# Gate marks two expert units sooner, and the dot products of one token group spread anew, in a mixed-attention and expert-layer kernel

## The chip, the cores and the metric

The kernel runs on one core of one Trainium2 chip. The metric is the device time of one launch in microseconds. Besides the timed runs there is one profiled execution, whose rows are quoted below: PE is the matmul engine (PEld its weight loads), DVE the vector engine, ACT the scalar engine, POOL the GpSimd engine, SP the engine that only issues transfers.

## The reference

One layer: four attention branches over 512 tokens, a merge, a layer norm, and then the expert layer (PEER) that this change is about. Cut to that:

```python
q = (xt @ wq).reshape(t_len, 8, 2, 64)
sub = einsum('thpd,hpkd->thpk', q, subkeys)        # 128 keys per half
s_top, i_top = top_k(sub, 16)
cand = s_top[:, :, 0, :, None] + s_top[:, :, 1, None, :]
sc, ci = top_k(cand.reshape(t_len, 8, 256), 16)
eid = (i1 * 128 + i2)                               # 8 heads x 16 = 128 experts a token
gate = softmax(sc, axis=-1)
h = gelu(einsum('cd,ced->ce', xc, u[eid]))          # u: 16384 x 1024
out = einsum('ce,ced->cd', gate * h, v[eid])
```

Everything is float32; the kernel splits each float32 operand into a high and a low part and adds three products.

## The kernel before

**Two ways through the expert layer.** Tokens 128 to 511 (three groups of 128) are computed densely: 128 "expert units" multiply all 16384 rows of `u` with the 384 tokens, 24 matmuls a unit (three per 128 columns, lines 1444 to 1446). After each unit ACT applies gelu (`gelu_of`, L776) and stores 192 KB of it to memory (`gelu_d`, L788); the store of unit j has to land before the gelu of unit j + 2 may write the same buffer (L785). The last eight units, 120 to 127, keep their gelu on the chip and store nothing. Then 128 "value units" multiply gate times gelu with `v`. Tokens 0 to 127 go another way: for each of their 128 picks one row of `u` per token is gathered by POOL (`get_u`, L535, an indirect transfer of 512 KB) and DVE takes a dot product with it (`dot`, L1168). The dot products have no dependence on the matmuls of the units, and are spread over the units as filler for DVE.

**Routing and marks.** DVE finds the picks of each token group (`route(b)`), b = 0 first and then 1, 2, 3. `route` calls `between` after each of its steps, 21 times in all, and there the dot products and marks of the previous stretch are slipped in (`next_units`, L1400). When route(b) is done, PE turns the picks round (three transposes, `turn_picks`, L1800) behind the unit before `MARK_AT[b]`, DVE copies them (`spread_picks`, L1290), and then a gate table for the 384 tokens is built eight tokens at a time: DVE makes a one-hot pair `hits` and `right` (`mark`, L1303), and PE multiplies them (`gates_of`, L1806, 16 matmuls a group, between two units). There are 48 such groups, 16 for each b. ACT copies the result to `stage` and, when four groups are full, stores four pieces of 512 KB to `gate_d` (`store_gates`), one piece a unit. For the last four groups it stores all four pieces at once, behind unit `TAIL`.

**What sets the order.** `MARK_AT` holds the unit at which each stretch of marks starts, and (entry 4, `TAIL`) the one after its end: `groups_in(j)` says which groups belong to unit j. `DOT_PACE` holds how many dot products are done by which unit; `dots_by(j)` (L84) interpolates between its points. PE, DVE, ACT and POOL all unroll their order from these tables:

- DVE does route(1) in the units 16 to `MARK_AT[1]` - 1, route(2) in the first stretch of marks, route(3) in the second.
- POOL makes the low part of each unit's weights (`expert_lo(k)`, L528, for unit k + 2) and between two of them issues gathers. The first 15 rows use three buffers, one row a unit; from `MARK_AT[1]` on it issues up to `dots_by(k - 1) + 5` rows before `expert_lo(k)`, in five buffers. Each gather waits until the dot product that last used its buffer is done (L535 and following), and row 15 also for the end of route(1). In a unit with a group, POOL waits in addition for that group's `right` (L570).
- ACT runs the exponent of each group's gates at a fixed unit, with a table load ahead of it and one behind it (`gate_exp`, L821, called at L838).
- SP loads the weights of the units one after the other, and after that of unit 125 the first part of the gate table.

```python
for k in range(FIRST_UNITS, MARK_AT[1]):
    expert_lo(k)
    rows_to(min(EARLY, k - FIRST_UNITS + 1))
for k in range(MARK_AT[1], P):
    rows_to(dots_by(k - 1) + U_SLOTS)
    if groups_in(k):
        pool.wait_ge(right_set, groups_in(k).stop)
    expert_lo(k)
```

Of the kernel before, what the change touches and what calls it, by code (L numbers as in the profile page):

```python
# [25 lines left out]
P = 128  # L26
# [43 lines left out]
GATE_SCALE = 2.0 ** 15  # L70
FIRST_UNITS = 16
STEPS = 22
MARK_AT = {1: 31, 2: 62, 3: 93, 4: 115}
TAIL = MARK_AT[4]
DOT_PACE = ((FIRST_UNITS + 5, 0), (MARK_AT[1], 14), (MARK_AT[2], 49), (MARK_AT[3], 84), (TAIL, 114), (P - 3, P))
EARLY, EARLY_SLOTS = 15, 3
U_SLOTS, V_SLOTS = 5, 6
FMA_START, FMA_END = 2, P - 12
# [5 lines left out]
def dots_by(k):  # L84

    for (k0, n0), (k1, n1) in zip(DOT_PACE, DOT_PACE[1:]):
        if k < k1:
# [4 lines left out]
def groups_by(b, k):  # L92

    return P // MARKED * (b - 1) + P // MARKED * k // (MARK_AT[b + 1] - MARK_AT[b])


def groups_in(j):

    b = marking_at(j)
    return range(groups_by(b, j - MARK_AT[b]), groups_by(b, j - MARK_AT[b] + 1)) if b else range(0)  # L100

# [7 lines left out]
def marking_at(j):  # L109

    return sum(j >= MARK_AT[b] for b in range(1, NT)) if j < TAIL else 0

# [87 lines left out]
def peer_block(nc, xT, x_rows, w_units, u_units, v_rows, u_rows, sinks, ln1_g, ln1_b, subk, ln2_g, ln2_b,  # L200
# [182 lines left out]
    with nc.Block() as block:  # L383
# [90 lines left out]
        def _(pool):  # L474
# [53 lines left out]
            def expert_lo(k):  # L528

                n = U_EXP + k + LO_AHEAD  # L530
                pool.wait_ge(hi_done, n + 1)
                pool.tensor_tensor(w_lo[:, n % RAW, :], raw[:, n % RAW, :], w_hi[:, n % RAW, :].bitcast(F32),  # L532
                                   ALU.subtract).then_inc(lo_pool, 1)
# [21 lines left out]
            def rows_to(n):  # L555
                while got[0] < min(n, P):
                    get_u(got[0])
                    got[0] += 1
# [4 lines left out]
            rows_to(EARLY_SLOTS)  # L563
            for k in range(FIRST_UNITS, MARK_AT[1]):
                expert_lo(k)
# [1347 lines left out]
```

## Time and profile before

| what | value |
|---|---|
| median of 3 runs | 1657.44 us (1654.45 to 1659.41) |
| the profiled execution's own time | 1661.09 us |
| its span | 1659.4 us |
| PE busy | 1636.9 us, 99% of the span |
| DVE / ACT / POOL busy | 74% / 42% / 51% |
| mean granted PE clock | 0.997 |
| chain that ended last | PE 86%, DVE 8%, DMA 2% |

PE is busy for nearly the whole span, so what a change is worth is read from the few gaps between its matmuls and from the stretches in which its clock is not full. All times below are in us from the start of the span. The expert units run from about 544 to 1128.

### The profile page before, as it was taken

The page shows a single profiled execution, that of the slowest core. Times are in us where ns is not written, and L with a number is a line of the kernel's source. Part 1 is how long each engine was busy: PE and PEld are TensorE (multiplying, and loading weights), DVE is VectorE, ACT ScalarE, POOL GpSimd, SP SyncE. Part 2 cuts the span into 40 slices and gives each one's busy share as a digit, 9 for nine tenths or more (in the row PEclk, how much of TensorE's full clock was granted, in tenths as well). Part 3 has the DMA queues.
Part 4 walks back from the last instruction along what each step waited for, and adds up shares of the span by engine and source line. Part 5 has one row for each costly group of instructions (what it writes and reads, how often), then busy time and mean ns, then how long its engine had stood idle before and what let it go on. Part 6 is the DMA issues. An engine that isn't in the chain of part 4 may idle for free.

```text
span 1659.4 us, 24178 instructions
## 1 busy us (share of the span) xinstructions
PE 1636.9 (99%) x9013; PEld 1436.7 (87%) x9013; DVE 1230.8 (74%) x2375; ACT 692.4 (42%) x1030; POOL 840.6 (51%) x492
## 2 busy tenths in 40 slices
PE   9999999999999999999999999999999999999997
PEld 7778777788889999999999999998888888888886
DVE  3586895512162988999899978736988888888886
ACT  4556545523233444444444544433333333333342
POOL 6232232444461568787887899873532233223212
PEclk9999999999999999999999999999999999999999
DMA  5121122233331568998999999999999999999952
GB/s 209 64 77 52 53 86 66 89 127 115 117 114 62 155 213 293 311 341 322 356 354 334 334 344 400 356 349 357 399 394 356 361 386 357 370 386 346 387 186 89
DMA packets 131684, 417.62 MB, mean 252 GB/s; under 512 B 13552, under 2 KB 33008, under 8 KB 131568
## 3 DMA queue, kind: packets, MB, share of 16 engines
q1 hardware_dynamic: 70320, 232.81, 40.0%
q0 software_dynamic: 36864, 134.23, 21.8%
q10 hardware_dynamic: 24384, 49.03, 7.7%
q8 instruction: 72, 1.18, 0.3%
q14 instruction: 44, 0.36, 0.1%
HBM read 364.91 MB, written 50.86 MB: 251 GB/s over the span
## 4 chain that ended last, share of the span: by engine, by line
PE 86%; DVE 8%; DMA 2%; ACT 1%; POOL 1%; issue 1%; ACTq 0%; SPq 0%; DVEq 0%
PE ps L1444 16%; PE ps L1445 16%; PE ps L1446 16%; PE ps L1706 10%; PE ps L1703 10%; PE ps L1704 10%; PE ps L1815 2%; DVE u_got L1168 1%; DVE hits L1311 1%; PE ps L1556 1%; PE ps L1508 1%; DMA gelu_d<-gelu_t 1%; POOL w_lo L488 1%; PE ps L1539 1%; DVE right L1318 1%
## 5 line engine op out<-in xcount | busy, mean ns | idle before, releaser
L1444 PE MATMUL ps<-tok_hi,w_hi 128*128 128x384 f32 (+1 forms) x1472 | 526.3, 358 | 4.0 <-ACT gelu_t L786 3.7
L1446 PE MATMUL ps<-tok_hi,w_lo 128*128 128x384 f32 (+1 forms) x1472 | 517.7, 352 | 0.0
L1445 PE MATMUL ps<-tok_lo,w_hi 128*128 128x384 f32 (+1 forms) x1472 | 517.6, 352 | 0.0
L595 ACT ACTIVATE w_hi<-raw 128x1024 fp32r<-128x1024 f32 x330 | 349.2, 1059 | 396.8 <-PE ps L1706 293.0
L532 POOL TENSOR_TENSOR w_lo<-raw,w_hi 128x1024 fp32r<-128x1024 f32 x128 | 312.8, 2444 | 109.1 <-ACT w_hi L595 66.6
L488 POOL TENSOR_TENSOR w_lo<-raw,w_hi 128x1024 fp32r<-128x1024 f32 x76 | 182.0, 2399 | 314.7 <-ACT w_hi L595 314.5
L1444 PEld LDWEIGHTS ps<-tok_hi,w_hi 128*128 128x128 f32 x1472 | 276.7, 188 | 34.1 <-issue 10.3
L549 POOL DMA_INDIRECT v_got<-v_rows,eid x128 | 153.1, 1196 | 300.9 <-DVE own L1180 283.7
L1703 PE MATMUL ps<-w_hi,gh_hi 128*128 128x512 f32 x760 | 295.7, 389 | 0.0
L1704 PE MATMUL ps<-w_lo,gh_hi 128*128 128x512 f32 x760 | 295.7, 389 | 0.0
L1446 PEld LDWEIGHTS ps<-tok_hi,w_lo 128*128 128x128 f32 x1472 | 276.9, 188 | 18.1
L1445 PEld LDWEIGHTS ps<-tok_lo,w_hi 128*128 128x128 f32 x1472 | 277.1, 188 | 16.0
L1706 PE MATMUL ps<-w_hi,gh_lo 128*128 128x512 f32 x760 | 234.0, 389 | 0.0
L1162 DVE TENSOR_TENSOR w_lo<-raw,w_hi 128x1024 fp32r<-128x1024 f32 x126 | 156.4, 1241 | 74.3 <-ACT w_hi L595 74.2
L1168 DVE CUSTOM_DVE_ANT_0 u_got<-u_got,ps 128x1024 f32<-128x1024 f32 x128 | 153.0, 1216 | 50.0 <-DMA u_got<-u_rows,eid 47.3
L1706 PEld LDWEIGHTS ps<-w_hi,gh_lo 128*128 128x128 f32 x760 | 142.6, 188 | 29.7
L1703 PEld LDWEIGHTS ps<-w_hi,gh_hi 128*128 128x128 f32 x760 | 142.7, 188 | 29.6
L1704 PEld LDWEIGHTS ps<-w_lo,gh_hi 128*128 128x128 f32 x760 | 142.6, 188 | 29.6
L541 POOL DMA_INDIRECT u_got<-u_rows,eid x128 | 155.5, 1215 | 25.0 <-issue 15.8
L1180 DVE SCALAR_TENSOR_TENSOR own<-v_got,w_own,own 128x1024 f32<-128x1024 f32 x126 | 160.0, 1279 | 0.0
L786 ACT ACTIVATE gelu_t<-ps 128x384 f32<-128x384 f32 x120 | 59.1, 492 | 228.6 <-PE ps L1446 211.8
L1311 DVE TENSOR_TENSOR hits<-numbers,mark_keys 128x2048 f16<-128x2048 f16 x48 | 94.8, 1974 | 0.8
(248 smaller groups left out, 1782.2 us busy)
## 6 DMA issues: line engine op xcount, KB each, us to landing
raw<-u_units SPq DMA_DIRECT2D x128, 512.0 KB
raw<-v_rows SPq DMA_DIRECT2D x128, 512.0 KB
raw<-w_units SPq DMA_DIRECT2D x78, 512.0 KB
gate_d<-stage ACTq DMA_DIRECT2D x48, 512.0 KB
gelu_d<-gelu_t ACTq DMA_DIRECT2D x120, 192.0 KB
gelu_in<-gelu_d SPq DMA_DIRECT2D x30, 768.0 KB, 8.1
gate_in<-gate_d SPq DMA_DIRECT2D x28, 768.0 KB, 12.3
gate_in<-gate_d SPq DMA_DIRECT2D x2, 1536.0 KB, 12.3
```

Source lines behind the costliest of these rows:

```text
L488: pool.tensor_tensor(lo_of(n), raw[:, n % RAW, :], hi_of(n).bitcast(F32), ALU.subtract).then_inc(lo_done, 1)
L532: pool.tensor_tensor(w_lo[:, n % RAW, :], raw[:, n % RAW, :], w_hi[:, n % RAW, :].bitcast(F32), ALU.subtract).then_inc(lo_pool, 1)
L595: act.activation(hi_of(n), raw[:, n % RAW, :], ACT.Copy).then_inc(hi_done, 1)
L1162: dve.tensor_tensor(w_lo[:, n % RAW, :], raw[:, n % RAW, :], w_hi[:, n % RAW, :].bitcast(F32), ALU.subtract).then_inc(lo_dve, 1)
L1168: dve.tensor_tensor_reduce(out=u_got[row_slot(e)][:], in0=u_got[row_slot(e)][:], in1=ps[:, 6:8, :].rearrange("p a n -> p (a n)"), scale=1. ...
L1180: dve.scalar_tensor_tensor(own[e % 2][:], v_got[e % V_SLOTS][:], w_own[:, e:e + 1], own[e % 2][:], ALU.mult, ALU.add).then_inc(fma_done, 1)
L1444: pe.matmul(out_, l_hi, r_hi, start=start, stop=False)
L1445: pe.matmul(out_, l_hi, r_lo, start=False, stop=False)
L1446: return pe.matmul(out_, l_lo, r_hi, start=False, stop=stop)
L1703: pe.matmul(o, l_hi[:, tile_], wh, start=start, stop=False)
L1704: pe.matmul(o, l_hi[:, tile_], wl, start=False, stop=False)
L1706: last = pe.matmul(o, l_lo[:, tile_], wh, start=False, stop=stop)
```

## The change

Each stretch of marks starts two units sooner (29, 60, 91 in place of 31, 62, 93) and the last one ends two units sooner (its last group at unit 112 in place of 114). The points of `DOT_PACE` hang on `MARK_AT`, so they move with it, and each count is 3 lower: 11 dot products by unit 29 (14 by 31 before), then 35, 35 and 30 in the stretches (as before), and 17 in the last 15 units (14 in the last 13 before). `EARLY`, the number of buffers, and every instruction are as they were; only the order changes. The names used elsewhere are unchanged.

```diff
-MARK_AT = {1: 31, 2: 62, 3: 93, 4: 115}
+MARK_AT = {1: 29, 2: 60, 3: 91, 4: 113}
 TAIL = MARK_AT[4]
-DOT_PACE = ((FIRST_UNITS + 5, 0), (MARK_AT[1], 14), (MARK_AT[2], 49), (MARK_AT[3], 84), (TAIL, 114), (P - 3, P))
+DOT_PACE = ((FIRST_UNITS + 5, 0), (MARK_AT[1], 11), (MARK_AT[2], 46), (MARK_AT[3], 81), (TAIL, 111), (P - 3, P))
```

POOL around the start of the marks, before. The rows begin with the low part of unit 30's weights (`expert_lo(28)`); u_got_143 to u_got_145 are the three buffers of the first rows, with 146 and 147 the five of the later ones.

```order
L532 TENSOR_TENSOR w_lo<-raw,w_hi 128x1024
L541 DMA u_got_143<-u_rows,eid 128x1024
L532 TENSOR_TENSOR w_lo<-raw,w_hi 128x1024
L541 DMA u_got_144<-u_rows,eid 128x1024
L532 TENSOR_TENSOR w_lo<-raw,w_hi 128x1024
L541 DMA u_got_145<-u_rows,eid 128x1024
L541 DMA u_got_146<-u_rows,eid 128x1024
L541 DMA u_got_147<-u_rows,eid 128x1024
L541 DMA u_got_143<-u_rows,eid 128x1024
L541 DMA u_got_144<-u_rows,eid 128x1024
L532 TENSOR_TENSOR w_lo<-raw,w_hi 128x1024
```

POOL at the same place, of the change; the first row is again the low part of unit 30.

```order
L532 TENSOR_TENSOR w_lo<-raw,w_hi 128x1024
L541 DMA u_got_143<-u_rows,eid 128x1024
L541 DMA u_got_144<-u_rows,eid 128x1024
L541 DMA u_got_145<-u_rows,eid 128x1024
L541 DMA u_got_146<-u_rows,eid 128x1024
L532 TENSOR_TENSOR w_lo<-raw,w_hi 128x1024
L541 DMA u_got_147<-u_rows,eid 128x1024
L532 TENSOR_TENSOR w_lo<-raw,w_hi 128x1024
```

Behind the low part of unit 30, rows 12 to 15 (buffers 143 to 146) now stand together ahead of the low part of unit 31. Before, row 12 and row 13 each stood before one low part, and rows 14 to 18 together ahead of that of unit 33.

DVE at the end of route(1), before: from the last step of the routing (L1286 sets the picks) to the first group of marks (L1311, L1318). Each L1168 pair is one dot product.

```order
L1286 TENSOR_TENSOR pick<-pick,g_sum 128x128
L1168 ISA u_got_145,h_own<-u_got_145,ps 128x1024
L1168 ISA h_own 128x1
L1168 ISA u_got_143,h_own<-u_got_143,ps 128x1024
L1168 ISA h_own 128x1
L1168 ISA u_got_144,h_own<-u_got_144,ps 128x1024
L1168 ISA h_own 128x1
L1296 CAST mark_keys<-ps 128x256
L1297 TENSOR_SCALAR mark_gates<-ps 128x64x2
L1299 SCALAR_TENSOR_TENSOR mark_gates<-ps,mark_gates 128x64x2
L1192 MAX s_top<-sub 128x8 x8
L1168 ISA u_got_145,h_own<-u_got_145,ps 128x1024
```

This piece is word for word the same in the change; its dot products are those of rows 8, 9, 10 and, behind the copy of the picks, 11, where before they are 11, 12, 13 and 14. Route(1) itself holds 8 dot products in the change and 11 before, since three of them drop out of its steps: here is one place of the difference.

```order
 L1268 TENSOR_TENSOR sub<-c_row,ps 128x2048
-L1168 ISA u_got_145,h_own<-u_got_145,ps 128x1024
-L1168 ISA h_own 128x1
-L1168 ISA u_got_143,h_own<-u_got_143,ps 128x1024
-L1168 ISA h_own 128x1
 L1272 TENSOR_TENSOR sub<-sub,ps 128x2048
+L1168 ISA u_got_144,h_own<-u_got_144,ps 128x1024
+L1168 ISA h_own 128x1
 L1275 TENSOR_REDUCE pick<-sub 128x128
```

ACT behind the last group of marks (`stage` is the copy of the gates, `gate_d` the four pieces stored at once): the difference.

```order
 L801 ACTIVATE stage_138<-ps 128x128x4 x2
 L809 DMA gate_d<-stage_138 128x1024 x4
+L595 ACTIVATE w_hi<-raw 128x1024
+L786 ACTIVATE gelu_t<-ps 128x384
+L788 DMA gelu_d<-gelu_t 128x384
+L595 ACTIVATE w_hi<-raw 128x1024
+L786 ACTIVATE gelu_t<-ps 128x384
+L788 DMA gelu_d<-gelu_t 128x384
 L595 ACTIVATE w_hi<-raw 128x1024
 L786 ACTIVATE gelu_t<-ps 128x384
```

Two more gelus, each with a store, follow the four pieces: six (units 114 to 119) in place of four (116 to 119) before the units that store nothing.

## Rows read from the trace of the kernel before

**Rows 1.** The page's first part: busy time and share of each engine.

```profile
PE 1636.9 (99%) x9013; PEld 1436.7 (87%) x9013; DVE 1230.8 (74%) x2375; ACT 692.4 (42%) x1030; POOL 840.6 (51%) x492
```

**Rows 2.** PE's waits by releaser, the longest: us in total, times, longest.

```profile
PE ps L1444 <- ACT gelu_t L786: 3.7, 1, 3.7
```

**Rows 3.** Stretches: busy us (instructions) of each engine, clock, DMA share, GB/s.

```profile
588.00:661.50 73.50, 73.50 (x426) 73.50 (x426) 63.35 (x239) 29.94 (x40) 55.74 (x31) 1.00 0.81 263
...
677.00:762.00 85.00, 84.42 (x580) 82.59 (x579) 83.61 (x251) 37.58 (x55) 68.06 (x39) 1.00 0.93 331
```

**Rows 4.** Timeline of PE: start, us, operation [idle before <- releaser].

```profile
668.42 0.49 PE L1803 MATMUL ps<-ident,pick 128*128 128x128 f32 x3
...
676.92 0.34 PE L1446 MATMUL ps<-tok_hi,w_lo 128*128 128x384 f32 x1
677.31 1.09 PE L1815 MATMUL ps<-right,hits 128*128 128x128 f16 x16
...
761.02 0.34 PE L1446 MATMUL ps<-tok_hi,w_lo 128*128 128x384 f32 x1
761.88 1.10 PE L1815 MATMUL ps<-right,hits 128*128 128x128 f16 x16 [0.53 <-DVE right L1318]
```

**Rows 5.** Timeline of DVE, end of route(1) and first marks.

```profile
625.23 1.22 DVE L1168 CUSTOM_DVE_ANT_0 u_got<-u_got,ps 128x1024 f32<-128x1024 f32 x1 [7.93 <-DMA u_got<-u_rows,eid]
...
659.23 2.34 DVE L1286 TENSOR_TENSOR pick<-pick,g_sum 128x128 f32<-128x128 f32 x1
...
668.27 1.22 DVE L1168 CUSTOM_DVE_ANT_0 u_got<-u_got,ps 128x1024 f32<-128x1024 f32 x1 [3.14 <-DMA u_got<-u_rows,eid]
...
669.42 0.42 DVE L1296 CAST mark_keys<-ps 128x256 f16<-128x256 f32 x1
...
671.96 1.21 DVE L1168 CUSTOM_DVE_ANT_0 u_got<-u_got,ps 128x1024 f32<-128x1024 f32 x1
...
676.03 1.22 DVE L1318 TENSOR_TENSOR right<-hits,mark_gates 128x2048 f16<-128x2048 f16 x1
```

**Rows 6.** Timeline at the start of the third stretch, PE and then DVE.

```profile
958.90 0.49 PE L1803 MATMUL ps<-ident,pick 128*128 128x128 f32 x3
...
959.43 0.42 DVE L1296 CAST mark_keys<-ps 128x256 f16<-128x256 f32 x1 [4.74 <-issue]
```

**Rows 7.** Timeline of POOL around the start of the marks.

```profile
659.01 2.40 POOL L532 TENSOR_TENSOR w_lo<-raw,w_hi 128x1024 fp32r<-128x1024 f32 x1
661.57 0.95 POOL L541 DMA_INDIRECT u_got<-u_rows,eid  x1 [0.16 <-issue]
...
667.59 0.94 POOL L541 DMA_INDIRECT u_got<-u_rows,eid  x1 [0.30 <-issue]
668.84 0.93 POOL L541 DMA_INDIRECT u_got<-u_rows,eid  x1 [0.31 <-issue]
```

**Rows 8.** Timeline of ACT and its queue behind unit 115.

```profile
1072.09 0.49 ACT L786 ACTIVATE gelu_t<-ps 128x384 f32<-128x384 f32 x1 [3.14 <-PE ps L1446]
...
1074.10 3.10 ACTq L809 DMA_DIRECT2D gate_d<-stage  x4
...
1078.77 0.33 ACTq L788 DMA_DIRECT2D gelu_d<-gelu_t  x1
...
1081.15 0.49 ACT L786 ACTIVATE gelu_t<-ps 128x384 f32<-128x384 f32 x1 [0.89 <-DMA gelu_d<-gelu_t]
...
1091.84 0.49 ACT L786 ACTIVATE gelu_t<-ps 128x384 f32<-128x384 f32 x1 [8.68 <-DMA gelu_d<-gelu_t]
```

**Rows 9.** Timeline of PE at the end of unit 119.

```profile
1088.36 0.34 PE L1446 MATMUL ps<-tok_hi,w_lo 128*128 128x384 f32 x1
1092.39 0.45 PE L1444 MATMUL ps<-tok_hi,w_hi 128*128 128x384 f32 x1 [3.69 <-ACT gelu_t L786]
```

**Rows 10.** The stretch behind that gap, columns as in rows 3.

```profile
1093.60:1097.00 3.40, 3.40 (x12) 3.40 (x11) 1.23 (x2) 1.80 (x3) 2.92 (x2) 0.50 1.00 330
```

**Rows 11.** Timeline of DVE ahead of the value units.

```profile
1120.19 0.56 DVE L1344 TENSOR_TENSOR gh_lo<-gh,gh_hi 128x384 fp32r<-128x384 f32 x1 [8.63 <-ACT gh_hi L851]
```

## The prediction

> **What bounds the kernel now.** I read the page's busy times first: PE is busy for 99% of the span [rows 1], so only three things can move the time: a gap between matmuls, a stretch at the lower clock, or a different number of matmuls. The change has the same instructions, so the third is out. The list of PE's waits comes next: the longest of all is one wait of 3.7 us for a gelu [rows 2]. Then the timeline of PE, for the place and size of each gap in the expert units [rows 4, 9]. A unit is 24 matmuls and takes (1088.70 - 1072.05) / 4 = 4.16 us, from the end of unit 115 (ACT's gelu behind it starts at 1072.09 [rows 8]) to that of unit 119 (1088.36 + 0.34 [rows 9]): one matmul starts 0.17 us behind the other. What is beyond that is lost:
>
> - At unit 32, with the first group of marks: 676.92 to 677.31, less 0.17: 0.22 us.
> - At unit 50: 761.02 to 761.88, less 0.17: 0.69 us, waiting for `right`.
> - Ahead of unit 120: 1088.36 to 1092.39, less 0.17: 3.86 us, waiting for ACT's gelu of unit 118. Behind it, from 1093.6, stand 3.40 us at a granted clock of 0.50, which is 1.2 GHz of the 2.4 [rows 10]; they hold half the work, so they cost 1.70 us. Together 5.56 us.
>
> So there is 0.91 us at the start of the marks and 5.56 us in the tail to win, and whatever is delayed by more than its slack to lose. From 677 to 762 DVE is busy for 83.61 of 85 us [rows 3]: in the first stretch it has no room, and its work there starts with the copy of the picks.
>
> **The front: picks and marks two units sooner.** PE asks for the picks of group 1 not at 668.42 [rows 4] but at 668.42 - 8.32 = 660.1. DVE had them at 659.23 + 2.34 = 661.6 [rows 5]. With nothing else changed, PE would wait 1.5 us. But route(1) now holds 8 dot products and not 11, each 1.15 us to the next instruction (668.27 to 669.42 [rows 5]): 3.45 us less, and the picks are there at 658.1, 2 us ahead. Besides, DVE idled for 73.5 - 63.35 = 10.2 us of that stretch [rows 3], 7.93 of it for row 3 [rows 5]. POOL issues these rows at the same units as before and the dot products stand later in the routing, so DVE is there later and waits less; of the 10.2 us I take 6 to 7 away: picks at about 652. The dot products of rows 8, 9 and 10 follow. Row 13 was issued at 661.57 [rows 7] and used at 668.27, 6.7 us later; row 10 goes out three units sooner, at some 649 to 651, and is there by 657.5. So DVE is free before 659 and waits for the transposes. At the third stretch, where it waited too, the copy starts 959.43 - 958.90 = 0.53 us behind the first transpose [rows 6]; at the first stretch it was 669.42 - 668.42 = 1.00, because the dot product at 668.27 was late by 3.14 us [rows 5]. In the change the copy then starts at 660.1 + 0.53 = 660.6, 0.47 us sooner against PE. From the copy to the end of the first `right` are 676.03 + 1.22 - 669.42 = 7.83 us: 668.5. PE comes to that group 676.92 + 0.17 - 668.42 = 8.67 us behind its transposes, at 668.8: no wait. Up to unit 50 DVE has the same instructions from the copy on, so the 0.91 us that PE lost shrinks by 0.47 to about 0.44. **Gain 0.47 us.** Bounds: 0.91 if both gaps go; a loss of 0.4 if DVE's waits don't shrink, since the three dot products then end at 658.1 + 3.45 = 661.5, 0.9 behind 660.6.
>
> **POOL at the same place.** This is a wait that the change adds. Ahead of the low part of unit 31 now stand rows 13, 14 and 15, and row 14 goes into the buffer of row 11, whose dot product stands behind the copy of the picks. It ends 671.96 + 1.15 - 669.42 = 3.69 us behind the start of the copy [rows 5]: 664.3. Until then POOL stands still, and the low part of unit 31, SP's load into the buffer that it frees, and all later gathers queue behind it. Then come rows 14 and 15 at 1.25 us each (667.59 to 668.84) and the low part of 2.40 us [rows 7]: 664.5 + 2.5 + 2.4 = 669.4. Unit 31 starts when unit 30 and the first group (1.09 us busy [rows 4], some 0.9 to 1.0 until the next unit's matmul) are done: 668.8 + 0.95 = 669.7. It fits by 0.3 us, where before this low part was ready at 659.01 + 2.40 = 661.4 [rows 7], over 7 us ahead. I take 0, the row nearest to it being on time; bounds 0 and 1 us. Unit 32 needs one row and one low part more: 669.4 + 3.65 = 673.1 against 669.7 + 4.16 = 673.9, and then the slack grows, since 3.65 us a unit is less than 4.16.
>
> **Exponent, middle.** ACT's exponent with its table loads moves with the marks to unit 24, which ends at 660.1 - 4 x 4.16 = 643.5; it has until DVE is within some 3 us of the picks (649), and it is three short instructions. From the second stretch on groups and dot products lie as before, two units sooner, and DVE has room there (4.74 us of idle at the third copy [rows 6]). 0 us for both; if that cover were gone, each us would be one on PE.
>
> **The tail.** Where the 3.86 us come from [rows 8]: behind unit 115 ACT issues the four pieces of 512 KB in one go (1074.10, 3.10 us), then the gelu store of unit 116 (1078.77). That lies behind 2 MB in the same queue and is landed at 1091.8, 13.0 us later; gelu 118 waits 8.68 us for it, and PE with it. In the change the pieces go out behind unit 113, and the store of unit 114 lies behind them. Dot products in the units that follow have the same sequence (1, 1, 2, 1, 2, 1, 1, 2, 1, 2), so the gathers on the DMA are the same too. With t for the end of the unit with the four pieces (1072.05), the store is issued at t + 6.7 and lands at t + 19.8, and PE wants the bank at t + 16.6: the same wait, ahead of unit 118. **Change 0 us**; bounds -5.56 (it lands 4 us sooner) and +5.2 (a rival below). The three dot products that came in end with unit 124 as before, and DVE idles 8.63 us ahead of the value units [rows 11], which hides them (3.45 us).
>
> One rule of the Trainium skill bears on the 1.70 us. The rows: behind 3.86 us of idle the clock fell to 1.2 GHz [rows 9, 10]. The page "TensorE: Matmul & The Clock Gate" (Part 1: The HAM clock gate) says that the activity window is free-running, so the same kernel shows different numbers of slow matmuls from run to run. By the row the moved gap costs the 1.70 again; by the rule it may cost none of it, and the sum would be 1655.3 in place of 1657.0. No run here shows which.
>
> **Sum.** The profiled execution took 1661.09 us (span 1659.4 and 1.7 around it): -0.47 at the marks, 0 elsewhere: 1660.6. It is 3.65 us over the median of the runs shown, which may be a part of the tail's 5.56. On the median: 1657.44 - 0.47 = **1657.0 us**.
>
> **Rivals.**
>
> *The tail wait goes.* For: the store before it landed 8.5 us after its issue (1072.6 to 1081.1 [rows 8]), and 13.0 need to fall by only 3.9. Against: the same 2 MB in the same queue. 1657.44 - 5.56 - 0.47 = 1651.4.
>
> *A second wait in the tail*, the one that ends slower. Before, the units behind the waiting gelu 118 are 119, behind which PE shows no gap, and 120, which stores nothing. In the change gelu 118 must wait for the store of unit 116, issued behind the first wait at t + 20.3. PE comes to unit 120 at t + 20.3 + 4.16 + 1.7 + 4.16 = t + 30.3. If the store takes 8.5 us, gelu 118 is done at t + 29.3, in time by 1 us; from 9.5 us on it is late, and at 13.0 it costs 3.5 us and 1.7 of slow clock: +5.2, less 0.47: 1662.2. For: the DMA's share there is 1.00 [rows 10]. Against: the 2 MB are gone by then.
>
> *POOL stands still too long on dot product 11.* It decides from 0.3 us on, and each us is one on PE at unit 31: with 1.5 us 1658.5.
>
> *The picks are late.* PE waits at unit 28, the 1.5 us worked out above: 1658.9. Against: the three dot products fewer.
>
> **How the numbers follow.** The forecast 0.62, the tail wait gone 0.15, the second wait 0.11, the two small delays 0.12 together. About 0.3% (5 us) is what a measurement of this kernel can tell from no change; the runs of before spread over as much. Below it lies only the first rival, with a little for parts unseen: faster 0.17. Above it only the second: slower 0.15. Same 0.68. Range 1652 to 1662: the forecast with the spread of the runs, the small delays, and part of each large case.
>
> **What would show it.** In the changed profile: the copy of the picks at about 660.6 with over 1 us of idle ahead of it; the first group, at unit 30, with no gap; the gap at unit 48 under 0.5 us; POOL's standstill on a dot product ahead of row 14, and unit 31 without a gap; ACT's wait for `gelu_d` of 5 us or more at gelu 116 and PE's gap of 3 to 4 us ahead of unit 118, with a stretch at 0.5 clock behind it. The prediction is wrong if PE has no gap over 2 us in the tail, or two, or if one over 1 us stands between units 28 and 33.

## The result and the profile after

| | median, us | lowest to highest | runs |
|---|---|---|---|
| before | 1655.56 | 1654.45 to 1659.41 | 22 |
| after | 1658.39 | 1656.63 to 1664.60 | 22 |

The ratio after to before is 1.0022, with a 95% interval of 1.0016 to 1.0028. By the medians the change is slower by 2.83 us (1.0017), by the means by 3.40 us, since six runs of after and none of before lie above 1660; the account below is of the medians. The loss lies inside the 0.3% that I had called no difference, but with this many runs it is clearly told from none, and it goes the other way than the 0.47 us that I forecast. One run of e8 and one of e15, below, took 4207 us in a slow state, and they stand outside the ratios and move those medians by some 0.02 us.

The number I started from was off as well. The median of the three runs shown was 1657.44; over 22 runs it is 1655.56. The profiled execution of before (1661.09) is 5.53 us above that: just the 5.56 us of [rows 8 to 10]. So the tail wait in the profile seems to belong to single runs and not to the typical one; e15 below bears that out (0.62 us of it in the median). The profiled execution of after (1658.28) is near its median.

The page's busy times and the list of PE's waits, after (answers to [rows 1, 2]; us in total, times, longest):

```profile
PE 1635.9 (99%) x9013; PEld 1436.4 (87%) x9013; DVE 1232.7 (74%) x2375; ACT 691.4 (42%) x1030; POOL 840.7 (51%) x492
...
PE ps L1815 <- DVE right L1318: 2.8, 2, 1.6
PE ps L1630 <- POOL ident L483: 1.6, 1, 1.6
PE ps L1444 <- DVE m_lo L1055: 1.4, 1, 1.4
PE ps L1444 <- ACT gelu_t L786: 1.2, 1, 1.2
```

The instructions are the same in number. Two waits on `right` have come, 2.8 us in all where there was one of 0.5, and the wait for a gelu is down from 3.7 to 1.2. PE's timeline, after (start, us, operation [idle before <- releaser]; answers to [rows 4, 9]):

```profile
659.18 0.49 PE L1803 MATMUL ps<-ident,pick 128*128 128x128 f32 x3
...
669.66 1.03 PE L1815 MATMUL ps<-right,hits 128*128 128x128 f16 x15 [1.65 <-DVE right L1318]
...
754.83 1.09 PE L1815 MATMUL ps<-right,hits 128*128 128x128 f16 x16 [1.12 <-DVE right L1318]
...
1082.84 0.44 PE L1444 MATMUL ps<-tok_hi,w_hi 128*128 128x384 f32 x1 [1.19 <-ACT gelu_t L786]
```

From start to start, less the 0.17 us of one matmul, the gaps are 1.81 us at the first group (0.22 before), 1.29 us at the tenth (0.69 before) and 1.36 us in the tail (3.86 before, with 1.70 of half clock). The two at the front make 3.10 us in place of 0.91: **+2.19 us**. Why the first `right` is late stands in the timelines of DVE and POOL, after (answers to [rows 5, 7]):

```profile
655.85 1.22 DVE L1168 CUSTOM_DVE_ANT_0 u_got<-u_got,ps 128x1024 f32<-128x1024 f32 x1 [3.67 <-DMA u_got<-u_rows,eid]
...
659.71 0.42 DVE L1296 CAST mark_keys<-ps 128x256 f16<-128x256 f32 x1 [2.62 <-PE ps L1803]
...
662.25 1.20 DVE L1168 CUSTOM_DVE_ANT_0 u_got<-u_got,ps 128x1024 f32<-128x1024 f32 x1
...
665.05 1.23 DVE L1311 TENSOR_TENSOR hits<-numbers,mark_keys 128x2048 f16<-128x2048 f16 x1
666.31 3.29 DVE L1318 TENSOR_TENSOR right<-hits,mark_gates 128x2048 f16<-128x2048 f16 x1
```

```profile
654.41 2.40 POOL L532 TENSOR_TENSOR w_lo<-raw,w_hi 128x1024 fp32r<-128x1024 f32 x1
...
658.22 0.94 POOL L541 DMA_INDIRECT u_got<-u_rows,eid  x1 [0.31 <-issue]
663.73 0.93 POOL L541 DMA_INDIRECT u_got<-u_rows,eid  x1 [4.57 <-DVE h_own L1168]
664.97 0.94 POOL L541 DMA_INDIRECT u_got<-u_rows,eid  x1 [0.30 <-issue]
665.93 2.58 POOL L532 TENSOR_TENSOR w_lo<-raw,w_hi 128x1024 fp32r<-128x1024 f32 x1
```

Row 14 waits 4.57 us for dot product 11. So the low part of unit 31 starts at 665.93, just ahead of `right` at 666.31, and `right` takes 3.29 us where it took 1.22 [rows 5]. It ends at 669.60, 1.09 us behind the end of POOL's instruction (668.51). Before, that low part ran from 659.01 [rows 7], and no POOL arithmetic lay beside the first `right` (676.03 to 677.25). POOL's low parts around it, before:

```profile
671.03 2.41 POOL L532 TENSOR_TENSOR w_lo<-raw,w_hi 128x1024 fp32r<-128x1024 f32 x1
...
677.33 2.40 POOL L532 TENSOR_TENSOR w_lo<-raw,w_hi 128x1024 fp32r<-128x1024 f32 x1 [2.78 <-DVE right L1318]
```

The tail, ACT and its queue, after (answers to [rows 8]):

```profile
1065.04 0.49 ACT L786 ACTIVATE gelu_t<-ps 128x384 f32<-128x384 f32 x1 [3.15 <-PE ps L1446]
...
1067.05 3.05 ACTq L809 DMA_DIRECT2D gate_d<-stage  x4
...
1071.67 0.33 ACTq L788 DMA_DIRECT2D gelu_d<-gelu_t  x1
...
1082.30 0.49 ACT L786 ACTIVATE gelu_t<-ps 128x384 f32<-128x384 f32 x1 [6.92 <-DMA gelu_d<-gelu_t]
```

The store behind the four pieces lands 10.6 us after its issue (1071.67 to 1082.3), where before's took 13.0. The wait is where I put it, and smaller.

### The profile page after: what moved, and what is told of

It reads as the page before. It is cut to its first block, busy times and chain, and to the rows that moved or that the text cites. A ratio compares the mean times of both kernels' runs of the same rounds, so it can differ in the third digit from the quotient of the medians.

```text
span 1656.5 us, 24176 instructions
## 1 busy us (share of the span) xinstructions
PE 1635.9 (99%) x9013; PEld 1436.4 (87%) x9013; DVE 1232.7 (74%) x2375; ACT 691.4 (42%) x1030; POOL 840.7 (51%) x492
## 4 chain that ended last, share of the span: by engine, by line
PE 91%; DVE 4%; DMA 2%; ACT 1%; POOL 1%; issue 0%; ACTq 0%; SPq 0%; DVEq 0%
PE ps L1444 18%; PE ps L1446 17%; PE ps L1445 17%; PE ps L1704 10%; PE ps L1706 10%; PE ps L1703 10%; PE ps L1815 3%; PE ps L1556 1%; PE ps L1508 1%; POOL w_lo L488 1%; PE ps L1539 1%; DMA gelu_d<-gelu_t 1%; DMA raw<-w_units 1%; DMA x_raw<-xT 0%; DVE right L1318 0%
## 5 line engine op out<-in xcount | busy, mean ns | idle before, releaser
L1168 DVE CUSTOM_DVE_ANT_0 u_got<-u_got,ps 128x1024 f32<-128x1024 f32 x128 | 153.1, 1216 | 44.9 <-DMA u_got<-u_rows,eid 44.3
L1311 DVE TENSOR_TENSOR hits<-numbers,mark_keys 128x2048 f16<-128x2048 f16 x48 | 95.1, 1982 | 0.8
```

## The experiments

Each was timed in five rounds beside the kernel before, on the same chip; the changed kernel was not timed in these rounds, so it is set beside them by its own +2.83 us over before. The intervals are about 1.5 us wide to either side, so a difference of medians below that is a hint, and the readings rest on the traces. The gaps are those of the one profiled run, whose time stands behind the median (from start to start, less 0.17 us): those of e3, e6 and e9 are 1.3, 2.7 and 3.4 us above their medians.

| run | marks; dots | median; profiled run | before there | ratio, 95% interval | gaps of PE: first group, tenth, tail |
|---|---|---|---|---|---|
| e1_front | 29, 60, 91, 115; 11, 46, 81, 114 | 1656.91; 1656.91 | 1655.34 | 1.0008, 0.9999 to 1.0017 | 1.81, 1.25, none |
| e2_tail | 31, 62, 93, 113; 14, 49, 84, 111 | 1655.01; 1656.48 | 1655.34 | 0.9997, 0.9988 to 1.0006 | 0.51, 0.72, 1.08 |
| e3_dots | 31, 62, 93, 115; 11, 46, 81, 111 | 1660.19; 1661.44 | 1655.34 | 1.0030, 1.0021 to 1.0039 | 1.82, 0.95, 2.50 and slow clock |
| e4_lofirst | as after | 1656.09; 1655.95 | 1655.34 | 1.0007, 0.9998 to 1.0016 | none, 0.81, 0.98 |
| e5_early14 | as after | 1657.64; 1657.15 | 1655.37 | 1.0013, 1.0004 to 1.0022 | none (1.11 at the second group), 1.45, 0.73 |
| e10_taildots | as before, 111 by the last | 1656.61; 1656.61 | 1655.66 | 1.0003, 0.9994 to 1.0012 | 0.59, 0.71, 0.59 |
| e6_spaced | as after | 1657.65; 1660.36 | 1655.66 | 1.0010, 1.0001 to 1.0018 | 1.81, 1.31, 1.30 and 1.19 |
| e8_best | as after | 1655.45; 1654.76 | 1655.66 | 1.0000, 0.9992 to 1.0009 | none, 0.83, none |
| e9_lofirst_114 | as after, 114 by the last | 1659.45; 1662.87 | 1655.66 | 1.0020, 1.0009 to 1.0032 | none, 0.79, 3.74 and slow clock |
| e13_gelu4 | as after | 1656.91; 1656.91 | 1655.37 | 1.0011, 1.0002 to 1.0020 | 1.81, 1.23, none |
| e15_before_gelu4 | as before | 1654.75; 1655.01 | 1655.37 | 0.9993, 0.9984 to 1.0003 | 0.28, 0.71, none |
| e14_front_gelu4 | as e1 | 1654.66; 1654.86 | 1655.37 | 0.9998, 0.9989 to 1.0007 | none, 0.84, none |

**The change in its parts: e1, e2, e3.** Each is the kernel before with other numbers in the two tables.

```diff
 e1:
+MARK_AT = {1: 29, 2: 60, 3: 91, 4: 115}
+... (MARK_AT[1], 11), (MARK_AT[2], 46), (MARK_AT[3], 81), (TAIL, 114)
 e2:
+MARK_AT = {1: 31, 2: 62, 3: 93, 4: 113}
+... (MARK_AT[1], 14), (MARK_AT[2], 49), (MARK_AT[3], 84), (TAIL, 111)
 e3:
+MARK_AT = {1: 31, 2: 62, 3: 93, 4: 115}
+... (MARK_AT[1], 11), (MARK_AT[2], 46), (MARK_AT[3], 81), (TAIL, 111)
```

> The three starts of marks are moved two units sooner and the dot products of the first stretches lowered by 3 (29, 60, 91; 11, 46, 81), but the last group stays at unit 114 and the tail has 114 dot products by unit 115 as in the kernel before. Theory A (the low part of unit 31 on GpSimd, held back by dot product 11, falls on the first group's `right` on VectorE, which then takes 3.3 us in place of 1.2): the first group's `right` takes over 3 us, PE loses 1.5 to 2 us ahead of it and 1 to 1.5 us ahead of group 9, the time is 2.2 us over before (ratio 1.0013). Rival B (what is lost comes from the tail's stores two units sooner): ratio 1.000, and no gap over 0.7 us at the first groups.

> The first three starts and their dot products as before (31, 62, 93; 14, 49, 84); only the end of the last stretch is two units sooner (113, with 111 dot products by then). Theory A gives the front's gaps as before, 0.2 and 0.7 us, and for the tail a wait for the gelu store that comes in more of the runs: 0 to 2 us over before in the median (ratio 1.000 to 1.001), with single runs up to 8 us over. Rival B: the whole difference, ratio 1.0022.

> Marks where they were (31, 62, 93, 115), only the counts of dot products 3 lower in each stretch (11, 46, 81, 111). Theory A: here too row 14 waits on GpSimd for dot product 11, which now stands behind the copy of the picks; the low part of unit 33 starts at about 675 and the first group's `right` at 675.6, so it takes 3 us in place of 1.2, and PE loses 1.5 to 2 us at unit 32: ratio 1.0010 to 1.0014. Rival C (it is the earlier time of the marks that costs, the picks or the first group being late on VectorE): the front as before or better, ratio 1.000.

PE's waits on `right`, of e1 and then of e2:

```profile
PE ps L1815 <- DVE right L1318: 2.7, 2, 1.6
```

```profile
PE ps L1815 <- DVE right L1318: 0.9, 2, 0.6
```

e1 has the whole loss of the front (1.82 and 1.25 us), and e2 next to nothing of it (0.51 and 0.72, where before has 0.22 and 0.69). In its timed runs e1 is 1.57 us over before where 2.2 was expected; its trace has no gap in the tail, and what before's tail costs (e15 below, 0.62) makes up the difference. e2 is 0.33 us under before and none of its runs is above 1656.5, the profiled one with its tail gap of 1.08 us being the slowest: the two units alone, moved at the end of the last stretch, lose nothing, and the single runs up to 8 us over that I expected did not come. e1 and e2 add up to 1.24 us, the whole change costs 2.83: the two halves don't add.

e3 has the loss of the front although no mark of the first three stretches has moved. POOL and DVE of e3:

```profile
672.82 0.95 POOL L541 DMA_INDIRECT u_got<-u_rows,eid  x1 [5.75 <-DVE h_own L1168]
674.08 0.94 POOL L541 DMA_INDIRECT u_got<-u_rows,eid  x1 [0.30 <-issue]
675.04 2.57 POOL L532 TENSOR_TENSOR w_lo<-raw,w_hi 128x1024 fp32r<-128x1024 f32 x1
```

```profile
674.14 1.23 DVE L1311 TENSOR_TENSOR hits<-numbers,mark_keys 128x2048 f16<-128x2048 f16 x1
675.40 3.29 DVE L1318 TENSOR_TENSOR right<-hits,mark_gates 128x2048 f16<-128x2048 f16 x1
```

The same picture, 9 us later: it is the dots by the first mark (11 in place of 14) and not the sooner marks that make the gap. Row 14 needs the buffer of row 11 here too, and the low part that it pushes (675.04) is now that of unit 33. e3 is slower than expected all the same: 4.85 us over before and not 1.7 to 2.3. The front's gaps hold 1.86 us (1.82 + 0.95 - 0.91). Its profiled run, 1.25 us above its median, has besides a tail wait of 2.50 us and slow clock behind it (columns as in [rows 3]):

```profile
1092.90:1096.30 3.40, 3.40 (x11) 3.40 (x12) 1.93 (x3) 2.21 (x3) 2.35 (x2) 0.52 1.02 411
```

**The low part ahead of the rows: e4.** POOL's order at `MARK_AT[1]` alone is changed.

```diff
             for k in range(MARK_AT[1], P):
+                if k == MARK_AT[1]:
+                    expert_lo(k)
                 rows_to(dots_by(k - 1) + U_SLOTS)
 ...
-                expert_lo(k)
+                if k > MARK_AT[1]:
+                    expert_lo(k)
```

> The changed kernel, but GpSimd makes the low part of unit 31 ahead of rows 13 to 15 and not behind them. It still stands still on dot product 11, only with nothing but row transfers behind it. Theory A: the low part runs from about 657 to 659.4, the first group's `right` takes 1.2 us, the gap at unit 30 is under 0.3 us and the one at unit 48 0.2 to 0.8 us: 1.8 to 2.4 us less than the changed kernel, ratio to before 1.0005 (what the tail costs). Rival C: no difference to the changed kernel, 1.0022.

POOL and DVE of e4:

```profile
658.26 2.39 POOL L532 TENSOR_TENSOR w_lo<-raw,w_hi 128x1024 fp32r<-128x1024 f32 x1
...
664.05 0.94 POOL L541 DMA_INDIRECT u_got<-u_rows,eid  x1 [2.29 <-DVE h_own L1171]
...
667.94 2.39 POOL L532 TENSOR_TENSOR w_lo<-raw,w_hi 128x1024 fp32r<-128x1024 f32 x1 [0.47 <-DVE right L1321]
```

```profile
666.63 1.22 DVE L1321 TENSOR_TENSOR right<-hits,mark_gates 128x2048 f16<-128x2048 f16 x1
```

Row 14 still waits for dot product 11, until the same time (664.05 against 663.73), but nothing but gathers runs beside `right`, which is back at 1.22 us; the first gap is gone and against before the loss is 0.75 us in place of 2.83, about the 0.8 expected. So the standstill is harmless, and the instruction that it pushes is not.

**A fifth buffer sooner: e5.** `EARLY` 14 in place of 15, so that row 14 goes into a buffer not used yet.

> The changed kernel with EARLY 14 in place of 15: row 14 goes into a fifth buffer that is still unused, so POOL doesn't wait there for dot product 11, which stands behind the copy of the picks. Rows keep their order and so do the low parts. Theory A (the loss at the front is POOL's wait for that buffer, which puts the low part of unit 31 beside the first group's hits and right): POOL issues rows 13 to 15 without a wait of over 1 us, the low part of unit 31 is done by 662 as in the order with the low part first, the first right takes 1.2 us, PE's gap at unit 30 is 0.4 us at most, and the median is 1656.0 to 1656.9, some 1.8 us below the changed kernel's. Rival C (DVE is late of itself, by its own work ahead of the first group): the gap at unit 30 stays over 1.5 us and the median at 1658.4. A gain of only 1 us would say that the wait has moved to row 15 or 16, in the next buffers.

A miss in size: e5 is 2.27 us over before, so 0.56 us is won and not 1.8. The low part of unit 31 is done at 664.2, later than the 662 expected but 2.2 us ahead of the first `right`, which takes 1.22 us, and PE has no gap at the first group. But the wait has only moved on to row 16, which needs the buffer of row 12, as the expectation allowed for. POOL and DVE of e5:

```profile
661.75 2.41 POOL L532 TENSOR_TENSOR w_lo<-raw,w_hi 128x1024 fp32r<-128x1024 f32 x1
669.03 0.95 POOL L541 DMA_INDIRECT u_got<-u_rows,eid  x1 [4.87 <-DVE h_own L1168]
...
673.53 2.42 POOL L532 TENSOR_TENSOR w_lo<-raw,w_hi 128x1024 fp32r<-128x1024 f32 x1
```

```profile
666.39 1.22 DVE L1318 TENSOR_TENSOR right<-hits,mark_gates 128x2048 f16<-128x2048 f16 x1
...
674.13 2.92 DVE L1311 TENSOR_TENSOR hits<-numbers,mark_keys 128x2048 f16<-128x2048 f16 x1
677.08 1.23 DVE L1318 TENSOR_TENSOR right<-hits,mark_gates 128x2048 f16<-128x2048 f16 x1
```

Now POOL's low part from 673.53, that of unit 33, lies beside a later `hits`, which takes 2.92 us and ends 1.10 us behind it (677.05 against 675.95). PE waits at that group, the second, for 1.11 us:

```profile
678.36 0.81 PE L1815 MATMUL ps<-right,hits 128*128 128x128 f16 x11 [0.95 <-DVE right L1318]
```

**The dots of the tail: e10, and e9 with e4's order.** e10 is before with 111 dots by the last mark. e9 is e4 with 114.

```diff
 e10:
-... (MARK_AT[3], 84), (TAIL, 114), (P - 3, P))
+... (MARK_AT[3], 84), (TAIL, 111), (P - 3, P))
 e9:
-... (MARK_AT[3], 81), (TAIL, 111), (P - 3, P))
+... (MARK_AT[3], 81), (TAIL, 114), (P - 3, P))
```

> The kernel before with one number changed: 111 dot products by unit 115 and not 114, so 17 of them are left for the last units, at 1.7 a unit and not 1.4. Marks and front as before (gaps 0.2 and 0.7 us). Theory V: the gelu store behind the four pieces is late by 2 to 4 us more, PE waits ahead of unit 120 and its clock is halved behind it: 1657.5 to 1659, ratio 1.0013 to 1.0022. Rival W: ratio 1.000.

> As the run with the low part first, but 114 dot products by unit 113 and not 111, so three of them leave the tail and 14 are left. Theory V (what makes the store late in more of the runs is the three rows more, 1.5 MB, that are gathered behind the four pieces): the tail's gap goes in most runs, median 1654.8 to 1655.3, none above 1657. Rival W (it is the two gelus more that have to wait for a store): as with the low part first alone, 1656.1, with single runs near 1660.

The three rows more in the tail don't explain what is lost there. e9 takes them out again and is 3.79 us over before, where e4 is 0.75 over it, which neither theory had; e10 puts them in and is 0.95 us over, with an interval that holds 1, half of what theory V wanted at the least. The runs of e9 spread from 1654.9 to 1663.8, and the profiled one is near the upper end. PE of e9, and the stretch behind the gap (columns as in [rows 3]):

```profile
1084.62 0.69 PE L1447 MATMUL ps<-tok_hi,w_hi 128*128 128x384 f32 x1 [3.57 <-ACT gelu_t L789]
```

```profile
1084.70:1092.00 7.30, 7.30 (x26) 7.30 (x27) 2.46 (x4) 2.72 (x4) 5.36 (x4) 0.59 0.67 240
```

Its store of unit 114 took from 1071.83 to 1084.08, 12.3 us. e9 has 33 dot products in the 22 units ahead of the last mark, e4 has 30. That the denser gathers hold up the pieces would fit these two, but e3 has 30 as well and waits 2.5 us.

**The four pieces one a unit: e6, and e8 with e4's order.**

```diff
-                    if body == NB - 1 and j == table_ready(body):
-                        for part in range(STORES):
-                            store_gates(body, part)
-                    elif body < NB - 1 and 0 <= j - table_ready(body) < STORES:
+                    if 0 <= j - table_ready(body) < STORES:
 ...
+                if j < TAIL + STORES:
                     stores_at(j)
```

> The changed kernel, but the last four pieces of the gate table are stored one behind each of the units 113 to 116, not all at once behind 113. Theory T (the rest of the loss, beyond the 2.2 us at the first groups, is ScalarE's wait for a gelu store that stands behind 2 MB in its own queue): no gap of over 0.5 us ahead of any unit from 116 on, the front as in the changed kernel (1.8 and 1.3 us), the runs close together, 1656.9 (ratio 1.0009 to 1.0014). Rival U (the store is late because of the traffic of rows and weights, not for its place in the queue): the median stays at 1658.4, with single runs above 1660.

> The changed kernel with both: the low part of unit 31 ahead of rows 13 to 15, and the last pieces stored one a unit. If both losses are what theories A and T say, neither is left: gaps of 0.8 us together at the first groups, none in the tail, 1654.5 us, ratio to before 0.9990 to 0.9998. If one of them is not, 1656 or more.

e6 is 1.99 us over before, where the change is 2.83 over, and its trace, that of the slowest of its runs, still has two gaps of over 1 us in the tail, which theory T excluded; e8's trace has none, and it is 0.96 us under e4 by the same count, but 1 us above what was expected if both losses were gone. Both differences are smaller than the intervals. So the burst may be part of it, but waits remain, and another run had to take away the thing waited for.

**A gelu that doesn't wait: e13 and e15.** `gelu_t` four deep from unit 100 on, in space free by then; the only other edits are the four semaphores that go with it. e13 has it on the kernel after, e15 on before.

```diff
-                    if j >= 2:
-                        act.wait_ge(gelu_out[j % 2], 16 * (j // 2))
-                    act.activation(gelu_t[:, j % 2, :], ps[:, j % 2, 0:DT], ACT.Gelu)
+                    last = j - 2 if j < 102 else j - 4
+                    if last >= 0 and j not in (102, 103):
+                        act.wait_ge(gelu_out[last % 4], 16 * (last // 4 + 1))
+                    act.activation(gelu_t[j % 4 // 2 if j >= 100 else 0][:, j % 2, :], ...
```

> The changed kernel with gelu_t four deep instead of two from unit 100 on: a gelu then waits for the store four units back, and no longer for the one two units back. Nothing else moves. Theory T (what the change loses beyond the front, and the half clock of single runs, is the gelu's wait for its own buffer behind the four pieces of 512 KB): PE has no gap over 0.3 us between units 113 and 124 and no stretch at half clock, gelu 116 waits for no store, the runs lie closer together than the changed kernel's (1656.6 to 1664.6), and the median is 0.5 to 1 us lower, 1657.4 to 1657.9; the gaps at the first and the tenth group stay at 1.8 and 1.3 us. Rival L (the DMA engines themselves are full behind the four pieces, and the loads of the units come late with or without the buffer): a PE gap over 1 us between units 116 and 122 that ends at a split of raw, median 1658.4 as the changed kernel.

> The kernel before with the same four-deep gelu_t from unit 100 on. Theory T: no PE gap over 0.3 us behind unit 115 and no half clock, as in the typical run of before; the gaps at units 32 and 50 stay (0.2 and 0.7 us); median 1654.7 to 1655.3. The difference to the changed kernel with the same buffers is then the front alone: 2.2 us (1.8 to 2.6). Rival L: gaps behind unit 115 stay, median as before's 1655.6, and the difference between the two kernels stays at 2.8.

ACT of e13 in the tail (the pieces, then the gelus of units 114 to 117):

```profile
1067.11 2.14 ACTq L810 DMA_DIRECT2D gate_d<-stage  x4
1070.32 0.47 ACT L787 ACTIVATE gelu_t<-ps 128x384 f32<-128x384 f32 x1
...
1073.42 0.49 ACT L787 ACTIVATE gelu_t<-ps 128x384 f32<-128x384 f32 x1 [1.11 <-PE ps L1447]
...
1077.58 0.49 ACT L787 ACTIVATE gelu_t<-ps 128x384 f32<-128x384 f32 x1 [2.15 <-PE ps L1447]
...
1081.74 0.49 ACT L787 ACTIVATE gelu_t<-ps 128x384 f32<-128x384 f32 x1 [2.15 <-PE ps L1447]
```

No gelu waits for a store, PE has no gap in the tail, and the runs span 1656.71 to 1658.13 where the changed kernel's spanned 1656.63 to 1664.60. The four pieces and the store behind them still take their time: the store issued at 1070.82 lands 11.7 us later, and nobody waits for it. So the units' loads are on time behind the burst (rival L is out), and the tail is this one wait. Each against before in its own rounds, e13 is at +1.54 and the change at +2.83: its tail costs 1.29 us in the median, and the trace of after, near the median, has a gap of 1.36 there. Before's own tail costs 1655.37 - 1654.75 = 0.62. And e13 less e15, two kernels without a tail wait in the same rounds, is 1656.91 - 1654.75 = **2.16 us, the front alone**; ten of the eleven runs of e15 (up to 1655.43) lie below all of e13's. The gaps of the traces gave 2.19, and e1, which has the front alone, is at 1.57 + 0.62 = 2.19 by the same count. That 2.16 + 1.29 - 0.62 gives 2.83 is no further proof, since all three come out of the same medians; the traces are the proof of the two parts.

**All of it together: e14.** The tables of e1, e4's order and e13's buffers.

> All that the runs before point to: marks 29, 60, 91, 115 (the last stretch as in the kernel before), dots 11, 46, 81, 114, the low part of unit 29 + 0 ahead of the rows issued in that unit, and gelu_t four deep from unit 100 on. By theories A and T no gap at the first group, 0.5 to 1 us at most at the tenth, none in the tail: 1654.3 to 1655.0, 0.3 to 1 us under the kernel before. By the rival that the marks' two units gain nothing and before's tail costs nothing in its typical run: 1655.6, the same as before.

At 1654.66 it is the fastest median of all. But 0.71 us under before has an interval that holds 1, and e15, with none of the sooner marks, is at 1654.75: the two units and the new dots are worth nothing that can be measured here.

## Why the prediction was wrong, point by point

- *The copy of the picks at 660.6, 0.53 us behind the transposes, with over 1 us of idle ahead.* Right: 0.53 us behind them (659.18 to 659.71) with 2.62 us of idle. PE as a whole was 0.9 us sooner than I had it. The picks were done at 649.9 (647.70 and 2.20) where I had 652, so the rival "picks late" is out.
- *"From the copy to the end of the first `right` are 7.83 us", so no wait at the first group.* **This is the step that failed.** It measured 669.60 - 659.71 = 9.89 us. I took `right` at the 1.22 us of [rows 5]; it took 3.29. The 2.07 us between them are the miss: PE waited 1.81, where by my sum the slack was 0.3. With the next gap below, the front lost 2.2 us where I had it win 0.47.
- *POOL stands still until 664.3, the low part of unit 31 is done by 669.4; "I take 0".* The mechanism was right and nearly to the number: 663.73 and 668.51, and unit 31 had no gap. But I asked only whether the moved instruction is on time for its own reader, and not what it now lies beside. My rival of POOL standing too long priced a late low part (1658.5, near the result) by a gap at unit 31; the price came through DVE, at unit 30.
- *The gap at unit 48 under 0.5 us.* Wrong: 1.29. e4 and e14, with the same sooner marks and the first `right` on time, have 0.8, so about 0.45 us of it goes with the first delay and 0.1 with the marks. e3, with the first delay and the marks unmoved, has 0.95, so the two don't simply add.
- *The tail: gelu 116 waits over 5 us, PE 3 to 4 us ahead of unit 118, half clock behind it; "Change 0 us".* Place right (6.92 us of ACT's wait), size wrong: 1.36 us, and full clock. I took 13.0 us for the store from one trace; it was 10.6 in this one, 9.1 in e1 (1079.83 to 1088.97), 11.7 in e3 (1080.49 to 1092.18) and 12.3 in e9. In the median the change's tail costs 0.67 us more than before's, against my 0. The two cases that I set for it, all 5.56 gone or 5.2 more, were both priced from one profiled run that stood 5.5 us above the median.
- *The second wait in the tail.* ACT did wait again (2.48 us, for the gelu at 1089.60), and PE did not.

The Trainium skill has the rule that I should have weighed. "SBUF — State Buffer" (section "Who interferes with whom") says that a DVE instruction with both inputs in SBUF contends with a GpSimd instruction that reads SBUF. By the summary of the same page of the Trainium skill (section "Summary: rules for kernel authors") the second of the two to issue is blocked until the first is done. The traces agree: `right` and `hits`, started while a low part ran, ended 1.09 us (after), 1.08 (e3) and 1.10 (e5) behind it, not much less than their 1.22 alone. The dot products read one input from PSUM; the one at 655.85, beside the low part of 654.41 to 656.81, took its usual 1.22. The kernel even has a wait that works as a guard: L570 holds a low part until the `right` of its group is set. But it stands only in units that hold a group: ahead of the low parts of units 32 and 34, not of 31, which before was done 14.6 us ahead of the first `right` (661.41 and 676.03), and not of 33, which met the first `right` in e3 and the second `hits` in e5.

As to the clock: behind the gap of 3.86 us of before the granted clock was 0.50 [rows 10], behind the 3.74 of e9 0.59 over the 7.3 us shown and behind the 2.50 of e3 0.52; behind the 1.36 and the 1.81 of after it stayed at 1.00. So the 1.70 us that I carried over went with the size of the gap; whether a gap as long as before's can cost none of it, no run here shows.

**Still open:** why the store behind the pieces lands after 10.6 us in one run and 13.0 in another, and why e3 and e9 wait so much longer there than e1 and e4 (some of that may be the profiled run, see the table). Nor is it shown why the tail costs 1.29 us behind the new front and nothing in e2 with the old one. e13 shows that the wait carries it, not what sets its length. One piece of it the semaphore updates of the traces show: the store is split into 16 shares, and in before the fifteenth landed at 1087.57 and the last at 1091.76, so 4.2 of the 13.0 us went on a single share; in after it is 2.3 us (1079.87 and 1082.21), in e3 0.7 and in e9 0.3.

## What to carry to other kernels

When a step is delayed and still in time for its reader, look at what runs beside it at its new place: here 4.6 us of waiting cost nothing by themselves, and the 0.4 us by which a POOL subtraction came ahead of a two-input DVE instruction cost 2.1. A guard against such a pair covers the order that it was written for; a table that moves rows can bring an unguarded instruction in. And before a gap of a profile is priced, compare the profiled run with the median: what lies between them, here 5.5 us, may be that very gap. The same holds for the traces of experiments.

## What the runs showed of the hardware

- A DVE `TENSOR_TENSOR` of 128x2048 f16 that takes 1.22 us alone took 3.29 when it began 0.38 us behind the start of POOL's 128x1024 subtraction. POOL's own instruction, which began while the `hits` before still ran (665.05 to 666.28), took 2.58 in place of 2.40. In the trace of after, 36 of the 96 `hits` and `right` began while a low part ran, and all of them ended 1.08 to 1.17 us behind it.
- A small lead doesn't help: in before a `right` that began 0.36 us ahead of a low part (1057.55 and 1057.91) took 3.84 us. In after all that led by 0.66 us or more kept their 1.22 to 1.23, and POOL's instruction took up to 2.82.
- Over the whole kernel after, `hits` takes 1.98 us in the mean and `right` 1.44, 48 times each, against 1.22 alone: (0.76 + 0.22) x 48 = 47 us of DVE, nearly all of it off the path.
- One store of 192 KB behind 2 MB in the same queue landed 10.6 to 13.0 us after its issue in the traces of before, after, e3 and e9, after 9.1 us in e1, and after 5.9 us in e14, all with the same burst of four pieces.
